# Moving one group of memory values to the front of a two-block transformer kernel, and re-timing the steps beside it

## What is computed

```python
# first layer: context and latent tokens, both modulated by a condition vector
sh, sc, g = split(silu(cond) @ ada_w[layer] + ada_b[layer], 3)   # "modulation"
xm = x * (1 + sc) + sh
q, k, v, o, z, gates, u, zp = split(xm @ w_in_even)               # context first, then latent
# second layer
v = layer_norm(v);  y = u * (w_sp @ v + b_sp) * silu(z)           # "sgu"
# larger block
h = rmsnorm(x, norm_mix);  rq, rk, rv, ... = split(h @ w_in)      # "ret_q" is the first part
mem_n = rmsnorm(mem, norm_mem)
K, V = mem_n @ xa_w_k, mem_n @ xa_w_v                             # memory keys and values
x = x + attention(rmsnorm(x) @ xa_w_q, K, V) @ xa_w_o
```

## Time and profile before

| | before |
|---|---|
| median of 3 runs | 3084.89 us |
| the profiled execution | 3085.91 us, its span 3084.1 us |
| PE busy | 3028.6 us (98%) |
| DVE busy | 2146.0 us (70%) |
| ACT busy | 1581.2 us (51%) |
| HBM read | 658.95 MB, mean 216 GB/s over the span |
| chain that ended last | PE 84%, DVE 8%, DMA 4%, ACT 2% |

### The profile page before, as it was taken

One profiled execution on the slowest core, in us unless ns is written; L12 is line 12 of the kernel. 1 busy time (PEld: TensorE's weight loads), 2 busy tenths in 40 slices (PEclk: granted clock), 3 DMA queues, 4 the chain that ended last, 5 costly groups with the idle time before them and its releaser, 6 DMA issues.

```text
span 3084.1 us, 44830 instructions
## 1 busy us (share of the span) xinstructions
PE 3028.6 (98%) x16750; PEld 2593.7 (84%) x16750; DVE 2146.0 (70%) x2720; ACT 1581.2 (51%) x1948; POOL 52.2 (2%) x52
## 2 busy tenths in 40 slices
PE   7899999999999999999999999999999999999998
PEld 5688878888788887888888888888888888888887
DVE  3389888788588787647668855566567777777554
ACT  3355444556544566444556654445345555555443
POOL 0032000000000000000000000000000000000000
PEclk9999999999999999999999999999999999999999
DMA  9966848786578656545555555575355555555554
GB/s 392 371 244 232 306 179 314 282 320 228 187 264 294 227 186 219 196 164 197 172 192 168 182 189 191 181 243 197 130 171 178 191 190 190 190 189 188 189 191 143
DMA packets 181403, 667.46 MB, mean 216 GB/s; under 512 B 20212, under 2 KB 20604, under 8 KB 179708
## 3 DMA queue, kind: packets, MB, share of 16 engines
q1 hardware_dynamic: 179580, 661.13, 62.2%
q10 hardware_dynamic: 1664, 4.19, 0.4%
HBM read 658.95 MB, written 6.30 MB: 216 GB/s over the span
## 4 chain that ended last, share of the span: by engine, by line
PE 84%; DVE 8%; DMA 4%; ACT 2%; DVEq 1%; issue 1%; SPq 0%; ACTq 0%
PE acc L791 45%; PE acc L795 22%; PE acc L802 4%; PE acc L804 4%; PE acc L803 4%; DVE w_lo L2060 3%; DMA mod_raw<-in_w_mod 2%; DVE mod_raw L2071 1%; DMA ada_more<-in_w_ada 1%; ACT w_hi L1314 1%; PE msc L839 1%; DMA raw<-in_w_xa_k 1%; PE acc L778 0%; PE msc L1210 0%; PE msc L1230 0%
## 5 line engine op out<-in xcount | busy, mean ns | idle before, releaser
L2060 DVE TENSOR_TENSOR w_lo<-raw,w_hi 128x1024 fp32r<-128x1024 f32 x1020 | 1241.3, 1227 | 597.7 <-ACT w_hi L1314 587.0
L1314 ACT CAST w_hi<-raw 128x1024 fp32r<-128x1024 f32 x1020 | 1061.3, 1048 | 835.6 <-PE acc L795 572.4
L791 PE MATMUL acc<-a_pair,w_hi 128*128 128x512 f32 x2944 | 929.7, 397 | 2.8 <-DVE w_lo L2060 1.6
L795 PEld LDWEIGHTS acc<-a_pair,w_lo 128*128 128x128 f32 x2944 | 553.0, 188 | 130.6
L791 PE MATMUL acc<-b_pair,w_hi 128*128 128x512 f32 x1792 | 569.9, 399 | 18.1 <-DVE w_lo L2060 18.1
L795 PE MATMUL acc<-a_pair,w_lo 128*128 128x256 f32 x2944 | 578.6, 278 | 0.0
L791 PEld LDWEIGHTS acc<-a_pair,w_hi 128*128 128x128 f32 x2944 | 450.3, 189 | 5.1 <-issue 1.9
L791 PE MATMUL acc<-f_pair,w_hi 128*128 128x512 f32 x1408 | 442.4, 395 | 0.0
L795 PEld LDWEIGHTS acc<-b_pair,w_lo 128*128 128x128 f32 x1792 | 337.2, 188 | 79.8
L795 PE MATMUL acc<-b_pair,w_lo 128*128 128x256 f32 x1792 | 352.8, 278 | 0.0
L795 PEld LDWEIGHTS acc<-f_pair,w_lo 128*128 128x128 f32 x1408 | 264.5, 188 | 62.5
(11 more groups left out here) (369 smaller groups left out, 2497.9 us busy)
## 6 DMA issues: line engine op xcount, KB each, us to landing
raw<-in_w_ffn_up SPq DMA_DIRECT2D x176, 512.0 KB, 4.0
mod_raw<-in_w_mod SPq DMA_DIRECT2D x128, 512.0 KB, 5.0
raw<-in_w_ffn_down SPq DMA_DIRECT2D x88, 512.0 KB, 3.3
ada_more<-in_w_ada SPq DMA_DIRECT2D x40, 512.0 KB, 14.2
raw<-in_w_xa_k SPq DMA_DIRECT2D x32, 512.0 KB, 12.6
raw<-in_w_k SPq DMA_DIRECT2D x32, 512.0 KB, 4.5
raw<-in_w_v SPq DMA_DIRECT2D x32, 512.0 KB, 5.6
raw<-in_w_even_out SPq DMA_DIRECT2D x32, 512.0 KB, 4.6
```

The source lines that it names most:

```text
L791: pe.matmul(acc[:, bank(stage, g) + m, :], w_h[:, cols], pair[:, :, kc, :], start=begin, stop=False, skip_group_check=True)
L795: mm = pe.matmul(acc[:, bank(stage, g) + m, 0:T], w_l[:, cols], pair[:, 0, kc, :], start=False, stop=end, skip_group_check=True)
L1314: nc.scalar.copy(w_hi[:, slot], source).then_inc(hi_done, 1)
L2060: vec.tensor_tensor(w_lo[:, slot], source, w_hi[:, slot].bitcast(F32), ALU.subtract).then_inc(lo_done, 1)
```

## The change

The first group of memory values becomes a stage of its own directly behind the keys (`mem_va`, 8 units). The other three groups shift: `mem_vb` (8 units) ahead of `sgu_v` and `mem_vc` (16 units, 24 before) ahead of `ret_q`. The quads are spread over all 32 key units (one at each odd step), the context is loaded behind the last quad, and the modulation and the context's pair move to steps 34 and 35 to 39, that is into the new stage, with step 7 of the pair still in `ctx_k`. With 16 units in place of 24 ahead of `ret_q`, the quarters, the column sums and the pair steps come closer together. Further, the high parts in the second layer come a step later, the last products of the later modulation are placed closer together, the mLSTM's first masks and scores come earlier and its table `top` is loaded in two halves, and the retention's scores leave out the half that is never read. The core of it:

```diff
-ADA_OVER = 24
+ADA_OVER = 32
     Stage("mem_k", "w_xa_k", "F", 1, groups=4, dve=1),
+    Stage("mem_va", "w_xa_v", "T", 1, groups=1),
     Stage("ctx_k", "w_k", "F", 1, gate=True, act=1, dve=1),
...
-    Stage("mem_va", "w_xa_v", "T", 1, groups=1),
+    Stage("mem_vb", "w_xa_v", "T", 1, groups=1, first_unit=DC // KU),
     Stage("sgu_v", "w_sgu_v", "T", 1, groups=4, act=1, woven=True),
...
-    Stage("mem_vb", "w_xa_v", "T", 1, groups=3, first_unit=DC // KU),
+    Stage("mem_vc", "w_xa_v", "T", 1, groups=2, first_unit=2 * DC // KU),
     Stage("ret_q", "w_ret_q", "F", 1, act=1, dve=1, woven=True),
...
-          ... "even_out": range(0, 24, 2), ...
+          ... "even_out": spread(20, 12), ...
-CTX_AT = STAGE["mem_k"].n - 5
-CTX_STEPS = {CTX_AT: (0,), CTX_AT + 1: (1, 2), CTX_AT + 2: (3,), CTX_AT + 3: (4, 5), CTX_AT + 4: (6,)}
-MOD_TURN = CTX_AT - 2
+CTX_AT = STAGE["mem_k"].n + 3
+CTX_STEPS = {CTX_AT: (0, 1), CTX_AT + 1: (2, 3), CTX_AT + 2: (4,), CTX_AT + 3: (5,), CTX_AT + 4: (6,)}
+MOD_TURN = CTX_AT - 1
-CTX_LOAD_AT = 23
-SGU_HIGH_AT = {at + 1: q for at, q in SGU_NORM_AT.items() if q < 8}
+SGU_HIGH_AT = {at + (1 if q < 2 else 2): q for at, q in SGU_NORM_AT.items() if q < 8}
-MIX_SUMS_AT = 17
-MIX_NORM_AT = 18
-NORMALISE_AT = {4: 0, 6: 1, 8: 2, 10: 3}
-SQUARES_AT = {5: 0, 7: 1, 9: 2, 11: 3}
-MIX_X_AT = {6: 0, 8: 1, 10: 2, 12: 3}
-QUARTERS_AT = {7: 0, 9: 1, 11: 2, 13: 3}
+MIX_SUMS_AT = 12
+MIX_NORM_AT = 13
+NORMALISE_AT = {4: 0, 5: 1, 7: 2, 9: 3}
+SQUARES_AT = {5: 0, 6: 1, 8: 2, 10: 3}
+MIX_X_AT = {7: 0, 9: 1, 11: 2, 13: 3}
+QUARTERS_AT = {6: 0, 8: 1, 10: 2, 11: 3}
-SCORES_AT = 13
-MASKED_AT = 14
+SCORES_AT = 12
+MASKED_AT = 11
...
                 def load_key(j):
-                    if j == CTX_LOAD_AT:
-                        sp.wait_ge(pe_step, BEFORE["mem_norm"]["pe"] + 1)
-                        nc.sync.dma_start(x[:], t["ctx"]).then_inc(ctx_in, 16)
...
+                for j in range(stage.n, stage.n + KEYS_AHEAD):
+                    for quad in ADA_AT.get(j - KEYS_AHEAD, ()):
+                        load_quad(quad)
+                sp.wait_ge(pe_step, BEFORE["mem_norm"]["pe"] + 1)
+                nc.sync.dma_start(x[:], t["ctx"]).then_inc(ctx_in, 16)
...
-                        if stage.name == "lat_q" and j == 6:
+                        if stage.name == "lat_q" and j in (6, 8):
                             sp.wait_ge(top_out, 16)
-                            nc.sync.dma_start(top[:].rearrange("p d h t -> p (d h t)"),
-                                              t["top"].rearrange("d h t -> (d h t)").partition_broadcast(P)).then_inc(top_in, 16)
+                            d = (j - 6) // 2
+                            nc.sync.dma_start(top[:, d].rearrange("p h t -> p (h t)"),
+                                              t["top"][d].rearrange("h t -> (h t)").partition_broadcast(P)).then_inc(top_in, 16)
...
             run("mem_k", b_pair, 0, batch=2, side=mem_sums)
+            run("mem_va", b_pair, PAIR["mem"], side=lambda j: mem_sums(STAGE["mem_k"].n + j))
...
-                            mm = pe.matmul(msc[:, h % 2, k * T:(k + 1) * T], kf[:, h, k * P:(k + 1) * P], qf[:, h, :],
+                            mm = pe.matmul(msc[:, h % 2, k * T + k * P:(k + 1) * T], kf[:, h, k * P:(k + 1) * P], qf[:, h, k * P:T],
                                            start=(k == 0), stop=True, skip_group_check=True)
```

More of the change, by code:

```diff
@@ L195 @@
           "lat_q": (0, 2, 4, 5, 7, 8, 10, 11, 13), "lat_o": spread(16, 12), "pool_u": spread(16, 9),
-          "mlstm_z": spread(16, 14), "pool_z": spread(16, 11), "even_out": range(0, 24, 2), "sgu_u": spread(32, 18), "sgu_z": spread(26, 14)}
+          "mlstm_z": spread(16, 14), "pool_z": spread(16, 11), "even_out": spread(20, 12), "sgu_u": spread(32, 18), "sgu_z": spread(26, 14)}
 MOD_PLACE = {}
@@ L1062, in row_sums @@
                     steps.done(mm)
-            run("sgu_v", b_pair, PAIR["mem_va"], batch=2, side=row_sums)
+            run("sgu_v", b_pair, PAIR["mem_vb"], batch=2, side=row_sums)
             def mix(j):
@@ L1095, in second_norm @@
                     steps.end("mix_pair")
-            run("mem_vb", b_pair, PAIR["mem_vb"], side=second_norm)
-            run("ret_q", a_pair, PAIR["mem_vb"], batch=2)
+            run("mem_vc", b_pair, PAIR["mem_vc"], side=second_norm)
+            run("ret_q", a_pair, PAIR["mem_vc"], batch=2)
             run("ret_k", a_pair, PAIR["mix"])
@@ L1543, in conv_silu, with values, group @@
                 return group
-            def values(i, g):
-                for tt in range(2):
-                    mm = nc.scalar.activation(va[:, tt, 2 * g:2 * g + 2, 0:MLSTM_D],
-                                              acc[:, 2 * g + tt, :].rearrange("p (h n) -> p h n", h=2), ACT.Copy, scale=0.5)
-                mm.then_inc(acc_free, 1)
-                act.drain()
-                ran(act.nop())
+            def values(name):
+                def group(i, g):
+                    first = bank(STAGE[name], g)
+                    for tt in range(2):
+                        mm = nc.scalar.activation(va[:, tt, 2 * g:2 * g + 2, 0:MLSTM_D],
+                                                  acc[:, first + tt, :].rearrange("p (h n) -> p h n", h=2), ACT.Copy, scale=0.5)
+                    mm.then_inc(acc_free, 1)
+                    act.drain()
+                    ran(act.nop())
+                return group
             def wide_and_last(j):
@@ L1589, in key_tokens @@
                     high(j - 9, 1)
-            run("ctx_v", values, side=key_tokens)
+            run("ctx_v", values("ctx_v"), side=key_tokens)
             def first_states(j):
@@ L1616, in exps @@
                     steps.end("lat_gates")
-            run("lat_v", values, side=exps)
+            run("lat_v", values("lat_v"), side=exps)
             def mlstm_exps(r):
@@ L1660, in output_gate @@
             def output_gate(i, g):
-                nc.scalar.activation(both, acc[:, 2 * (g % 2):2 * (g % 2) + 2, :].rearrange("p a b -> p (a b)"), ACT.Tanh,
+                first = bank(STAGE["lat_o"], g)
+                nc.scalar.activation(both, acc[:, first:first + 2, :].rearrange("p a b -> p (a b)"), ACT.Tanh,
                                      scale=0.5).then_inc(acc_free, 1)
@@ L1835, in halves @@
                 dve.add()
-            run("ret_q", lambda i, g: halves(qf, g), side=lambda j: mix_chunks(STAGE["mem_vb"].n + j))
+            run("ret_q", lambda i, g: halves(qf, g), side=lambda j: mix_chunks(STAGE["mem_vc"].n + j))
             run("ret_k", lambda i, g: halves(kf, g))
@@ L2337, in _ @@
             run("mem_k", none(), side=mem_chunks, dest=keys_out, scale=token_scale)
+            run("mem_va", none(), side=lambda j: mem_chunks(STAGE["mem_k"].n + j))
             def last_ctx(j):
@@ L2800, in rotated @@
                 return group
-            run("ret_q", rotated(qf), side=lambda j: mix_chunks(STAGE["mem_vb"].n + j), dest=in_slab(qf))
+            run("ret_q", rotated(qf), side=lambda j: mix_chunks(STAGE["mem_vc"].n + j), dest=in_slab(qf))
             run("ret_k", rotated(kf), dest=in_slab(kf))
```

23 lines of the change are left out of this document (12 added, 11 removed).

## The result

The changed kernel takes 3102.38 us (3097.02 to 3102.97, 5 runs) against 3084.89 (3082.85 to 3085.71, 5 runs): ratio 1.0052 [1.0041, 1.0063], 0.5% slower. The forecast was 3089.5 and its range ended at 3097. The profiled execution of after took 3102.38 as well, with a span of 3100.6 us, 16.5 more than the earlier trace rows. Two of the other executions took 3097.02 and 3098.61 us, so up to 5 us of what this one profile shows can vary from one execution to the next.

A forecast was written before the change was run, and what follows sets the result against it. PE is busy 98%, so the prediction took only the places where PE stands still as the question. 3085.9 - 24.1 of gains + 28.7 ahead of `ret_q` = 3090.5, less 1.0 to the median: 3089.5 us, range 3077 to 3097.

The forecast's parts named there:

- `even_out`, the step that failed: In `even_out`, the last three products come before the last chain, whose wait goes: 1.7 us less, bounds 0 and 2.5.
- two smaller ones stay: In `even_out`, two smaller waits were to remain once the 1.7 us wait with restart had gone.
- The stretch ahead of `ret_q`: Work of 24 units packed beside 16: column-sum and pair waits 21.2 plus clock 7.5, 28.7 us more, bounds 18 and 30.5.
- the clock, 7.5 for 9.5: Ahead of `ret_q`, PE at 1.2 GHz behind five new waits: 1.5 us each, 7.5 more, bounds 0 and 8.5.
- The start: Up to `ctx_k`, quads in time and PE setting the pace: `ctx_k` begins at 170.7, not 184.1, 13.4 us less.
- `ctx_k`: The context's pair: PE's wait for pair step 7, about 1.5 us with restart, goes: 1.5 us less.
- `sgu_v`: Second layer: high parts a step later end ACT's 2.50 us waits and five PE waits of 0.75: 3.7 us less.
- the retention's scores: 16 of 32 score instructions become half as long: 1.8 us less.
- `lat_q`: Scores ahead of unit 12 and earlier masks: 2.0 us less, bounds 0 and 3.5.
- the new waits weren't short: Rival: short waits ahead of `ret_q` and no clock fall at the three 3 us waits, loss 18 to 21, 3078; chance 0.2.
- the clock didn't stay up: Rival: only the clock stays up ahead of `ret_q`, loss 21 to 24, no change at 3082 to 3085; chance 0.2.
- the quads weren't late: Rival: at the start the quads come too late and PE waits, a loss of 8 us, 3097; chance 0.15.

The follow-up runs named there:

- Run 1: The changed kernel with the twelve products of `even_out` back at the even steps 0 to 22: 3094.25 us, ratio 1.0033.
- run 9: The changed kernel with `even_out`'s products of steps 17 and 19 moved to 20 and 22, behind the second chain: 3098.14 us, ratio 1.0042.
- run 5: The changed kernel with unread products sized to PE's new waits, 9 ahead of the column sums, 5 and three times 3 ahead of the pairs: 3090.22 us.
- run 4: The changed kernel with two pair steps of `ret_q` in each of four steps, not one in each of eight: 3086.64 us, ratio 1.0006.
- run 6: run 4 with column sums at step 13, the first pair steps in that step, and high parts either side of the store: 3077.49 us, ratio 0.9977.
- run 8: run 6 plus Run 1's edit, with the context's load issued in step 2 of the first value stage: 3071.09 us, ratio 0.9958.
- run 3: The changed kernel with unread products in PE's new waits, 20 ahead of the column sums, 8 and three times 6 ahead of the pairs: 3105.4 us.

## Why the prediction was wrong, step by step

The forecast for the median was 12.9 us too low. Of these 11.9 are in the steps below, and 1.0 is the step from the profiled execution to the median, which I took off and which after did not show.

**`even_out`, the step that failed: -1.7 forecast, +5.3 measured, 7.0 of the 12.9.** I wrote that the last three of twelve products come earlier, ahead of the chain of the earlier trace rows, that its wait goes, and that "two smaller ones stay". The first half holds: unit 29, behind the last chain, took 4.48 us before and 2.79 after, 1.7 less. The second half is where it failed. I read only the chain that PE waited for longest, and took the two others as they were, though the change moves a product onto each of them: the places of `spread(20, 12)` are plain in the diff, and laid beside the chains they show 14, 15, 17 and 19 around the second. After the change units 12 and 13 lose 1.8 more, unit 20 0.65 and unit 21 4.6 (8.23 in place of 3.64). Run 1 shows that it is this line; run 9 shows that the product of step 17 is 2.3 to 2.7 of it, about 1 itself and the rest the clock behind it. The size has luck in it: five profiles with this code in `even_out` lie between 94.5 and 98.0 us, 2.3 to 5.8 above the 92.2 before, and each one above it. My bounds for this edit, "0 and 2.5" of gain, had left out a loss without a reason that excludes it.

**The stretch ahead of `ret_q`: +28.7 forecast, +30.7 measured.** The mechanism was right wait by wait: 8.4 forecast for the column sums (8.7 with its restart), and 5.4 and three of 3.4 with hand-overs and restart of 0.5 in them; 8.23, 5.06, 3.05, 3.05 and 3.34 in the trace, without restart. Without the clock the forecast had 21.2; what run 5 leaves is 21.2 too. The term that was mis-sized is the clock, 7.5 for 9.5: I gave each slow stretch 1.5 us, but behind the 8.23 PE did 5.15 us of work at the lower level, worth 2.6, and behind the last wait 6.14 (from 1231.37 to 1237.51 the granted clock is 0.50), worth 3.1. The Trainium skill, "TensorE: Matmul & The Clock Gate", section "HAM oscillation — how this bites in real kernels", by whose rule I had 8.5, came nearer, though that too was reckoned with one price for every wait. That the waits follow from the order written down, one pair to a step, was argued; run 4 shows it for the three of 3 us (gone with two pairs to a step, 11.9 us less in `ret_q`), and run 6 for most of the rest.

**The start: -13.4 forecast, -10.4 measured.** The quads came in time, PE set the pace, and the two quads at half rate went. The 407 GB/s of the earlier trace rows, 410 here, carried it, where the 358 GB/s of the Trainium skill's "DMA: Bandwidth & Descriptors", section "Where 436 GB/s comes from", would have made them late; on one core the row was the right guide. 3 us are missing, and the trace places them: 1.4 ahead of the first value unit (the wait of 1.10 and its restart), 1.0 at one quad (0.96), 0.45 at the very start (quad 1 is used at 36.65 where the forecast had 36.2), and 0.2 at key unit 6, which takes 3.02 us and not 2.79 because PE turns the memory's scale there (L861), as it did before. I had the value weights "behind" the context's load and didn't price that; run 8 shows that the load's place costs 1.1. The first terms vary: the same code left this stretch between 172.05 us (run 9) and 173.94 (run 4).

**`ctx_k`, `sgu_v`, the retention's scores:** -1.5, -3.7 and -1.8 forecast, -1.5, -3.8 and -1.9 measured. These were read from a wait that recurs and has one cause. **`lat_q`:** -2.0 forecast, -3.4 measured; I had left out the slow stretch behind the 2.70, which I counted everywhere else.

**`ctx_v`, `lat_k`, `lat_v`:** nothing forecast, 1.4 us more. `lat_v` alone is 1.6 of it. It took 46.62 us in this profile, and 44.65 to 46.54 in the nine other kernels with the same code in it (runs 1 and 3 to 10), 45.00 before. The traces show where it comes from. In the changed kernel ACT waits 4.72 us for a weight load there and splits at 16.74 us after the stage's start, and DVE then waits 2.23 for the load of a product; in run 3, with the same code, it is 2.73 us, 14.76 and 1.64. Unit 10, which stands behind these, takes 4.05 us in the one and 2.75 in the other. Why the load lands at different times was not found, and no run was made for it.

**The rivals and the range.** None of the rivals came: the new waits weren't short, the clock didn't stay up, and the quads weren't late. The direction that I gave 0.30, slower, did not come by its rival: it came by `even_out`, the start and the clock ahead of `ret_q`, which all moved the same way; that rival had only late quads. And with every term at the bad end of its own bounds (+1.8 ahead of `ret_q`, +2.0 in `lat_q`, +1.7 in `even_out`) the sum would have reached only 3095.0: what lies beyond is the loss in `even_out`, for which no bound had been set, and the 3 us of the start, which had none either.

## What to carry to other kernels

When an edit shifts a set of small steps, lay all its new places beside every chain of the stage, not only beside the chain that it is meant to clear: the wait goes and comes back at the next one. When work is packed into fewer units by a fixed order, look for "one step per unit": each such step stands behind the use of the unit just before, so PE can't get ahead of it and waits each time, about 3 us here; two steps per unit gave back 11.9 us. Price a long wait of PE (here, from 3.05 us up) with the lower clock behind it, half of the work that PE does until it recovers, and not with its length alone; give the shorter ones, here from 1.78 us, a chance of that price. And compare several profiles of the same code before a difference of a few us is called the price of one edit.
